# Two transformer blocks on one core: five output-projection blocks by token halves, a ninth weight buffer pair, and three low parts per join on GpSimd

## The reference

```
h = h + rms_norm(mixed @ w_out, post_g)          # "out1" / "out2"
u = rms_norm(h, ffn_pre_g)                       # "x2" / "x4"
h = h + rms_norm(ffn(u), ffn_post_g)             # gate and up projections g1,u1 / g2,u2, then down
```

## Time and profile before

| | us |
|---|---|
| median of 3 runs (897.86 to 898.0) | 897.89 |
| the profiled execution | 897.94 |
| its span (first to last instruction) | 896.1 |

### The profile page before, as it was taken

How to read it: one execution, slowest core, us unless ns; L and a number is a source line. 1 busy time by engine, 2 the same in 40 slices (tenths; PEclk the granted TensorE clock), 3 DMA queues, 4 the chain that set the end, 5 groups by cost and what they waited for, 6 DMA issues and landing times.

```text
span 896.1 us, 16529 instructions
## 1 busy us (share of the span) xinstructions
PE 884.4 (99%) x6641; PEld 782.7 (87%) x6641; DVE 667.4 (74%) x1253; ACT 466.3 (52%) x940; POOL 200.4 (22%) x113
## 2 busy tenths in 40 slices
PE   9999999999999999999999999999999999999997
PEld 8879999989999798888888899977888888888886
DVE  7745987586447877786666767768888788788885
ACT  7444336665344774444444657866553545543443
POOL 4123421531132120553214522230001111210100
PEclk9999999999999999999999999999999999999999
DMA  8356453153424746555564374215354465465441
GB/s 331 114 184 234 140 174 112 48 212 142 142 96 145 278 163 236 188 196 187 187 219 169 124 247 165 97 48 211 142 222 161 182 213 204 152 230 188 174 156 48
DMA packets 23180, 153.66 MB, mean 171 GB/s; under 512 B 2864, under 2 KB 3248, under 8 KB 5568
## 3 DMA queue, kind: packets, MB, share of 16 engines
q1 hardware_dynamic: 22384, 150.44, 46.8%
q0 software_dynamic: 576, 2.10, 0.6%
q10 hardware_dynamic: 144, 0.07, 0.0%
HBM read 151.28 MB, written 1.05 MB: 170 GB/s over the span
## 4 chain that ended last, share of the span: by engine, by line
PE 96%; DVE 2%; ACT 1%; issue 1%; DVEq 0%; ACTq 0%
PE pb L528 94%; PE pb L531 2%; ACT FA L534 1%; DVE FA L537 0%; DVE wl L537 0%; ACT R L534 0%; DVE X L543 0%; DVE wh L552 0%; DVE FA L546 0%; ACT wh L534 0%; DVE FA L540 0%; DVE st L540 0%; DVE st L555 0%; DVEq L585 0%; DVE FA L543 0%
## 5 line engine op out<-in xcount | busy, mean ns | idle before, releaser
L528 PE MATMUL pb<-R,wh 128*128 128x256 f32 (+2 forms) x2224 | 545.5, 325 | 3.3 <-DVE R L543 2.0
L528 PE MATMUL pb<-R,wl 128*128 128x256 f32 (+1 forms) x1512 | 420.0, 281 | 0.0
L528 PEld LDWEIGHTS pb<-R,wh 128*128 128x128 f32 x2224 | 369.5, 188 | 43.3 <-ACT R L534 3.4
L537 DVE TENSOR_TENSOR wl<-raw,wh 128x1024 fp32r<-128x1024 f32 (+1 forms) x207 | 273.3, 1344 | 76.6 <-ACT wh L534 74.8
L537 POOL TENSOR_TENSOR wl<-raw,wh 128x1024 fp32r<-128x1024 f32 (+1 forms) x71 | 173.4, 2445 | 581.5 <-ACT wh L534 427.4
L528 PEld LDWEIGHTS pb<-R,wl 128*128 128x128 f32 x1512 | 283.4, 188 | 1.7
L534 ACT ACTIVATE wh<-raw 128x1024 fp32r<-128x1024 f32 (+1 forms) x223 | 226.1, 1044 | 52.0 <-PE pb L528 36.9
L528 PE MATMUL pb<-wh,R 128*128 128x512 f32 (+1 forms) x704 | 227.1, 389 | 0.1
L528 PEld LDWEIGHTS pb<-wh,R 128*128 128x128 f32 x704 | 131.7, 188 | 31.1 <-issue 1.7
L534 ACT ACTIVATE FA<-pb 128x256 f32<-128x256 f32 (+7 forms) x240 | 93.2, 411 | 118.4 <-PE pb L528 103.2
L528 PE MATMUL pb<-wl,R 128*128 128x512 f32 (+1 forms) x352 | 135.5, 385 | 0.0
(11 more groups left out here) (127 smaller groups left out, 434.6 us busy)
## 6 DMA issues: line engine op xcount, KB each, us to landing
raw<-in_w SPq DMA_DIRECT2D x137, 1024.0 KB, 4.8
X<-in_x SPq DMA_DIRECT2D x2, 512.0 KB, 4.1
raw<-in_w SPq DMA_DIRECT2D x2, 512.0 KB, 6.8
post<-in_ffn_post SPq DMA_DIRECT2D x2, 512.0 KB, 4.3
post<-in_w POOLq DMA_DIRECT2D x2, 512.0 KB, 4.9
FA<-in_w POOLq DMA_DIRECT2D x2, 512.0 KB, 8.0
out<-X SPq DMA_DIRECT2D x4, 256.0 KB, 2.0
cst<-in_cst SPq DMA_DIRECT2D x1, 822.5 KB, 12.6
```

Of the source, the lines that this page charges most:

```text
L528: return self.real.matmul(*a, **k) if self.real else self
L537: return self.real.tensor_tensor(*a, **k) if self.real else self
```

## The change

1. `TAILS` has the tail of out1 and out2 take five units (79 to 83, 175 to 179) and not four. The fourth `down` step goes (a dot less in `MIX`). In token half 0, tail (0,0) now also takes the first four units of column half 1; (0,1) is left with the last unit's 3 matmuls. (Before, only ffn2 did that.)
2. A ninth buffer pair (`ASIDE`), at columns 6144 to 8191 of FA, is used once per join, by the tail's last unit (83, 179), which so doesn't wait for TensorE to use up 79 (175). Its `split` becomes an "open" step among the side jobs (c in `MIX`) at about the same place. The square's unused output moves from FA 6144 on to FA 2048 on.
3. In `MADE` units 85, 86, 87 and 181, 182, 183 go from d to p: GpSimd makes their low parts. 87 and 183 leave `LATE`.
4. `gemm0` waits for the high parts only; `gemm1` waits for both.

```diff
+ASIDE = 8
+TAILS = dict(out1=5, ffn1=4, out2=5, ffn2=4)
@@ down_tail
-        units = p.weights(("tail", name), [(w, 128 * k, rng(128 * j)) for k in order[-4:] for j in range(8)])
+        units = p.weights(("tail", name), [(w, 128 * k, rng(128 * j)) for k in order[-TAILS[name]:] for j in range(8)])
@@ ffn
-        segs.append((down, main, [*chains(down, x), refill(units, list(range(first, first + NWIDE - NBASE)))]))
+        segs.append((down, main, [*chains(down, x), refill(units[:-1], list(range(first - 1, first + NWIDE - NBASE)))]))
@@ segments
-    for k in range(4):
+    for k in range(8 - TAILS["out1"]):
...
-    last, place, prior, after = {b: -NWIDE + b for b in range(NWIDE)}, [], [], {}
+    last, place, prior, after = {b: -NWIDE + b for b in range(NWIDE + 1)}, [], [], {}
...
+        if any(u == a - 1 for a, _ in wide):
+            b = ASIDE
@@
-MADE = ("dpdpddddddddqdpdpdddpddpvpvdppqpdddppddddpddvqpqpqpdpddddpdddpqddvdpddppddpddpddpddvvdddqdvdddpd"
-        "ddvvvdvdppdpdppvvpdqpdpqvddpvpdvpdddvpdvpdvdddvqdddqqpddpddqddvdddddddpvvvdppvpppdvvddddqdvddddd"
+MADE = ("dpdpddddddddqdpdpdddpddpvpvdppqpdddppddddpddvqpqpqpdpddddpdddpqddvdpddppddpddpddpddvvpppqdvdddpd"
+        "ddvvvdvdppdpdppvvpdqpdpqvddpvpdvpdddvpdvpdvdddvqdddqqpddpddqddvdddddddpvvvdppvpppdvvdpppqdvddddd"
@@ MIX
-    "out1": "............c.caac..aaacabab.bbaaaaaa.baaabbbcbbbbbbbbccc....",
+    "out1": "...........cc.caac..aaacabab.bbaaaaaa.baaabbbcbbbbbbbbccc....",
-    "out2": "c.caac..aaacabab.bbaaaaaa.baaabbbcbbbbbbbbccc....",
+    "out2": "cc.caac..aaacabab.bbaaaaaa.baaabbbcbbbbbbbbccc....",
@@
-LATE = {87: ('norm', 'out1', 0), 183: ('norm', 'out2', 0), 43: ('decay', 0, 6), 54: ('evac', 'qpe', 3), 154: ('scaled', 'ffn1', 0)}
+LATE = {43: ('decay', 0, 6), 54: ('evac', 'qpe', 3), 154: ('scaled', 'ffn1', 0)}
@@ program
-        sb("FA_low", 10672)
+        sb("FA_low", 6144)
+        aside = sb(f"wh{ASIDE}", 1024, FR), sb(f"wl{ASIDE}", 1024, FR)
+        sb("FA_mid", 10672 - 8192)
@@ opened
-            elif PLACE[u] >= NBASE and OPENS[1] <= u < OPENS[1] + NWIDE - NBASE:
+            elif PLACE[u] >= NBASE and OPENS[1] - 1 <= u < OPENS[1] + NWIDE - NBASE:
@@ tensor: gemm0
-                            unit(u)
+                            e.wait_ge(*(act if HI[u] == "act" else dve).at(("hi", u)))
@@ tensor: gemm1
+                            unit(u)
@@ tensor: tail
-                    if name == "ffn2" and c == 0:
+                    if name != "ffn1" and c == 0:
                         runs = [(j, k) for j in (0, 1) for k in ks[:-1] if h == 0] + [(h, ks[-1])]
@@ scalar: post
-                    e.activation(fa(6144 + 512 * (2 * c + h), 512), acc(name, c, h)[:, :], ACT.Square,
+                    e.activation(fa(2048 + 1024 * c + 512 * h, 512), acc(name, c, h)[:, :], ACT.Square,
```

More of the change, by code:

```diff
@@ L359, in segments @@
         p.tile("mk", n, True)
-    for k in range(4):
+    for k in range(8 - TAILS["out2"]):
         p.wide(("down", "out2", KORD2[k]), "w_out_2", KORD2[k], [rng(128 * j) for j in range(8)])
@@ L426 @@
     "latent": "..a......aaaaaaaa................bc....b.fgc.b..f.c.g..de.b.cf...d.gf.e.hi.dg.h.e.d..ie.h..i.h..i",
-    "out1": "............c.caac..aaacabab.bbaaaaaa.baaabbbcbbbbbbbbccc....",
+    "out1": "...........cc.caac..aaacabab.bbaaaaaa.baaabbbcbbbbbbbbccc....",
     "ffn1": "..aaaaac..acaba......aaaaaaaa....bbbbccbb......b.bbbb...bbbb............",
     "maps": "...a.....acbabcbc..cc.bbb.ede.eed.ecag.agcdgcggadc.b.bfcgbefdc.ab.dgfbe.dbhffbbhhhfa.ccccf.igecbeif."
-            "gahf.ddib.b.bbigchijbjj..cbhcibchkhajkhcikkhcjbiijbcijkijkcijg.kjjkk.ggkkij.k.",
-    "out2": "c.caac..aaacabab.bbaaaaaa.baaabbbcbbbbbbbbccc....",
+            "gahf.ddib.b.bbigchijbjj..cbhcibchkhajkhcikkhcjbiijbcijkijkcijg.kjjkk.ggkkij.k",
+    "out2": "cc.caac..aaacabab.bbaaaaaa.baaabbbcbbbbbbbbccc....",
     "ffn2": "aaaaa..bb.bbb.",
@@ L455 @@
 for _n, (_, _, _kt) in DOWN.items():
-    _ks = (KORD2 if _n == "out2" else list(range(_kt)))[-4:]
+    _ks = (KORD2 if _n == "out2" else list(range(_kt)))[-TAILS[_n]:]
     TAIL_AT.update({(_n, _k): BLOCK_AT["tail", _n] + 8 * _i for _i, _k in enumerate(_ks)})
@@ L618, in program @@
             WL.append(sb(f"wl{i}", 1024, FR))
+        WH.append(aside[0])
+        WL.append(aside[1])
         banks = Banks([ctx.enter_context(nc.psum_tensor(f"pb{i}", [128, 512], FP)) for i in range(8)])
@@ L1116, in tensor @@
                     name, c, h = a
-                    ks = (KORD2 if name == "out2" else list(range(DOWN[name][2])))[-4:]
+                    ks = (KORD2 if name == "out2" else list(range(DOWN[name][2])))[-TAILS[name]:]
                     runs = [(h, k) for k in ks]
-                    if name == "ffn2" and c == 0:
+                    if name != "ffn1" and c == 0:
                         runs = [(j, k) for j in (0, 1) for k in ks[:-1] if h == 0] + [(h, ks[-1])]
```

## The result

| | before | after |
|---|---|---|
| median, runs of one chip (6 each) | 898.07 us | 904.87 us (904.61 to 905.69) |
| the profiled execution | 897.94 us | 905.02 us |
| its span | 896.1 us | 903.2 us |

The ratio is 1.0077 (95% interval 1.0066 to 1.0088). The page of the changed kernel answers to the earlier trace rows: TensorE's busy time is up by only 2.1 of the 7.1 us by which the span grew, so most of the loss is idle TensorE, and a part of it is slower matmuls.

The account below looks back on a forecast made before the run. TensorE, busy 884.4 of 896.1 us, was taken to bound the kernel, so join delays stay to the end: 2.9 (join 1) + 3.6 (join 2) = +6.5 on 897.94 gave 904.4 us, range 897.8 to 905.6.

Parts of the forecast that it names:

- Mechanism A: Both joins: GpSimd's subtractions hold VectorE's casts, low parts and residual halves; 904.4 us (903.0 to 905.6), chance 0.47.
- B: Both joins: queued GpSimd doesn't part the residual halves, low 87 holds the scaling instead; +2.8, 900.7 us, chance 0.20.
- C: Both joins: GpSimd's subtractions miss the chain or leave the residual untouched; -0.6 to +0.6, 897.3 to 898.5 us, chance 0.27.
- Part 1: Five-block tail: 1.36 us more cover, some 0.3 reaching the chain; TensorE stops 0.5 us for unit 82.
- Part 2: Ninth buffer pair: earlier casts of units 83 and 179; gain bounded by 0.4 us, join 2's 0.3 us hole could go.
- Part 4: gemm0 waiting for high parts only: has to, with lows on GpSimd; gains 0, only bounds the damage.
- Join 1: First output projection to feed-forward join: GpSimd's holds delay residual halves, transposes (312.7 for 310.17) and gemm0; +2.9 us.
- Join 2: Second such join: 1 us tail stop, residual held, transposes some 3.4 us later, gemm1 3.6 later; +3.6 us.
- Rival E: gemm0 at each join: idle pauses of 2.5 us halve TensorE's clock to 1.2 GHz; about 912 us, chance 0.03.
- the lock: VectorE beside GpSimd: two-SBUF-input instructions wait for GpSimd's whole subtraction, queued GpSimd going ahead of the next; +6.5 us.

Follow-up runs that it names:

- e7: The changed kernel with the two residual halves made by one VectorE instruction of 1024 columns, all six low parts still on GpSimd: 902.33 us, ratio 1.0048.
- e1: The changed kernel with all six low parts back on VectorE, 87 and 183 late as before: 898.7 us, ratio 1.0005.
- e10: The changed kernel plus 7 unused matmuls of 512 columns just ahead of the transposes of half 0 at each join: 903.71 us, ratio 1.0063.
- e6: The changed kernel with only the low parts of 87 and 183 on GpSimd, the other four on VectorE: 904.58 us, ratio 1.0069.
- e5: The changed kernel with only the low parts of 86 and 182 on GpSimd, the others on VectorE: 898.5 us, ratio 1.0002.
- e2: The kernel before with only the six low parts given to GpSimd and gemm0 waiting for high parts only, old tail and buffers: 907.68 us, ratio 1.0108.

## Why the prediction was right, point by point

- **Mechanism A** happened as worked out. The rows I named: cast 84 was to end near 303.6 and did (303.64, or 303.4 with the shift off); the three subtractions were to end about 303, 307 and 310, and ended at 303.1, 307.7 and 310.5; a residual half was to take about 2.9 us, and the pair takes 4.37 = 1.42 + 2.95; transposes near 312.7, and they started at 312.76 with the shift off.
- **Rivals B and C** are out by the same rows: the scaling is its usual 0.49 us, and the residual form is held. B's price was well worked out, though: I gave +2.8 for halves not parted; the hold that is left in e7 (2.0) and the tail's 0.7 make 2.7.
- **Part 1**: the stop of 0.5 us for unit 82 came as 0.33 for unit 81, whose low part I hadn't looked at, and 0.45 for 82. "The sum of the tail's matmuls stays" was wrong by some 0.2 us per join, the 0.231 for 0.227 us of e1. The cover reached the chain no further than the end of the tail (e1). **Part 2**: bounded by 0.4; at join 2 the hole shrank from 0.28 to 0.10 us. **Part 4**: worth nothing, as I said, but "it has to" was wrong by my own instants (low 87 ready at 310.2, gemm0 at 314.8). In the changed kernel low 87 ends at 310.5 and gemm0 starts at 315.13, so there the old wait would have held nothing up.
- **Join 1** was given +2.9: without the clock's 1.1 us it is 3.90 - 1.09 = 2.8, of which e1 has 0.8 (tail, and the pause before gemm0 1.11 instead of 0.88) and GpSimd 2.0.
- **Join 2** was given +3.6 and came to 3.0: the step that was mis-sized. The residual's end was right (624.41, less 4.11 us of shift and loss so far, is 620.3; I had 620.4). But I then moved the transposes by the same 3.4 us as the residual. In the kernel before, 619.24 lies 2.24 us behind the residual's end at 617.0, since VectorE's low 183 holds up the reciprocal by 0.2 us and the transposes then wait for the tail's last matmul (619.01, the next start at 619.24); in the changed kernel it is 1.94, the 1.9 I had used in join 1. And the 0.2 us that I added for gemm0 were not there to add: its pause was already 1.11 us.
- **Rival E**, the clock, was given 0.03, because the clock never fell behind pauses of 0.9 us. It did fall, in join 1 only, to 0.50 from 316 to 318 and for a part of the slices beside: +1.1. As a case of its own, both joins in full, it was unlikely; as a term that comes on top of A with 1.8 us pauses, it should have been in A's range. The sum 6.5 was thus 0.7 too high in the lock (2.8 + 3.0 = 5.8) and 1.1 too low in the clock: that it came within 0.3 us of the measured 6.8 is in part luck, two errors that cancel. Without the clock's share the kernel measures 903.71 (e10), 0.7 below my 904.4.

| us, by gemm1's instants and medians | join 1 | join 2 | both |
|---|---|---|---|
| tail and ninth pair (e1) | 0.8 | -0.1 | 0.7 |
| hold by GpSimd's reads (after less e1, clock off) | 2.0 | 3.1 | 5.1 |
| TensorE's clock (after against e10) | 1.1 | 0 | 1.1 |
| sum | 3.9 | 3.0 | 6.9 |

**Open.** Why the clock fell in join 1 and not in join 2 of the changed kernel, behind equal pauses (1.83 and 1.09 us), no run here tells; e6's scatter shows that even one kernel differs from run to run. The tail of five without the ninth pair wasn't tried: its last unit would wait for a buffer that only later matmuls of the same tail free. Why matmuls follow one another 2% more slowly in the new tail is open too. None of the ten kernels is faster than the kernel before; e1 and e5 can't be told from it.

## What to carry to other kernels

Before work is moved to GpSimd, list the VectorE instructions with two SBUF inputs, and the casts, that will run beside it: each can be held for a whole GpSimd instruction, and two of them in a row twice, if GpSimd has the next one queued (here 2.95 us in all). Put GpSimd's reading work beside VectorE's PSUM work (low 86 alone, e5, cost nothing), or where VectorE's delay meets no one. And price a new TensorE pause like those here (1.5 to 4.1 us) twice: for itself and for a clock that may be halved behind it, 1.1 to 2.3 us for a join here.

## What the runs showed of the hardware that was not expected

- Between two VectorE instructions that follow back to back, without a wait, a queued GpSimd subtraction gets in: 4.37 us for a pair of 1.42, against 2.10 us for one instruction of the same columns (1.28 undisturbed).
- TensorE's clock was halved behind a pause of 1.5 to 1.8 us, transposes of 1.06 us and a second pause of 1.09 us (gemm0 5.54 us, in e6 once 6.74, for 4.28), but not each time; in e2 it was half already in the transposes behind a pause of 4.13 us. With 0.23 to 0.34 us in place of the first pause it stayed full (e7, e10). Seven unused matmuls bought back 1.2 and 2.3 us.
- GpSimd's memset holds VectorE's cast (1.24 us for 0.69) and is held by it in turn (1.38 us for 0.96), and leaves an instruction with two SBUF inputs alone.
- The 36 last matmul steps of the new tail take 8.33 us at full granted clock, 0.231 each for 0.227, with or without GpSimd beside them.
